# Gate and up tiles of the feed-forward stages: high weights times high and low activations in one 512-column product, the two parts added on VectorE

## The reference, cut to what matters

```python
def swiglu(h, wg, wu, wd):
    return (jax.nn.silu(h @ wg) * (h @ wu)) @ wd

for i in range(DEPTH):                         # DEPTH = 2
    ...
    x = x + swiglu(rms_norm(x, norm_ffn[i]), ffn_gate[i], ffn_up[i], ffn_down[i])
```

## Time and profile before

| | |
|---|---|
| median of 3 runs | 935.57 us (933.26 to 937.48) |
| the profiled execution | 935.31 us, its span 933.4 us |
| mean granted TensorE clock | 0.998 |
| PE busy | 914.7 us, 98% of the span, 7053 matmuls |
| DVE busy | 608.3 us, 65% |
| ACT busy | 485.7 us, 52% |
| POOL busy | 215.2 us, 23% |

### The profile page before, as it was taken

The page is one execution under the profiler, slowest core; times in us unless marked ns, Lnnn a source line. Parts: engine busy times, 40 slices in busy tenths (PEclk is TensorE's granted clock), DMA queues, the critical chain, the costliest instruction groups (busy, mean ns, idle before and its releaser), DMA issues.

```text
span 933.4 us, 17115 instructions
## 1 busy us (share of the span) xinstructions
PE 914.7 (98%) x7053; PEld 842.3 (90%) x7053; DVE 608.3 (65%) x827; ACT 485.7 (52%) x729; POOL 215.2 (23%) x177
## 2 busy tenths in 40 slices
PE   9999999999999999999999999999899999999998
PEld 8999999999999798899999997788788888899997
DVE  5876554554589999764545557746574756867664
ACT  6346434434465476744444346465556565547452
POOL 0005990000024230000000001316462704930100
PEclk9999999999999999999999999999999999999999
DMA  8765865666654522465656574546355635563461
GB/s 272 225 227 161 282 204 187 205 194 212 204 185 149 176 97 91 136 225 187 218 180 211 194 228 165 182 147 202 123 176 183 195 115 181 183 208 109 131 231 45
DMA packets 119636, 168.73 MB, mean 181 GB/s; under 512 B 5557, under 2 KB 88597, under 8 KB 119573
## 3 DMA queue, kind: packets, MB, share of 16 engines
q1 hardware_dynamic: 119140, 167.66, 55.5%
q10 hardware_dynamic: 432, 0.19, 0.1%
HBM read 165.38 MB, written 2.46 MB: 180 GB/s over the span
## 4 chain that ended last, share of the span: by engine, by line
PE 74%; DVE 14%; POOL 4%; ACT 3%; DMA 2%; issue 2%; SPq 0%; ACTq 0%; DVEq 0%; POOLq 0%
PE ps L480 21%; PE ps L482 21%; PE ps L481 21%; DVE wlo_sb L445 4%; POOL b_inv_sb L2477 3%; PE ps L922 2%; DMA raw_sb<-w_in_even 2%; PE ps L908 2%; PE ps L935 2%; DVE scratch_sb L1522 2%; ACT whi_sb L422 1%; POOL scratch_sb L2485 1%; PE ps L568 1%; DVE b_ss_sb L2319 1%; PE ps L2097 1%
## 5 line engine op out<-in xcount | busy, mean ns | idle before, releaser
L445 DVE TENSOR_TENSOR wlo_sb<-raw_sb,whi_sb 128x2048 fp32r<-128x2048 f32 x143 | 332.1, 2324 | 182.8 <-ACT whi_sb L422 182.7
L422 ACT ACTIVATE whi_sb<-raw_sb 128x2048 fp32r<-128x2048 f32 x143 | 273.6, 1914 | 161.8 <-PE ps L482 144.7
L480 PE MATMUL ps<-hhi_sb,whi_sb 128*128 128x256 f32 x992 | 274.1, 276 | 2.2 <-DVE wlo_sb L445 1.8
L481 PE MATMUL ps<-hlo_sb,whi_sb 128*128 128x256 f32 x992 | 272.8, 275 | 0.0
L482 PE MATMUL ps<-hhi_sb,wlo_sb 128*128 128x256 f32 x992 | 272.8, 275 | 0.0
L480 PEld LDWEIGHTS ps<-hhi_sb,whi_sb 128*128 128x128 f32 x992 | 190.4, 192 | 4.1 <-DVE wlo_sb L445 2.3
L481 PEld LDWEIGHTS ps<-hlo_sb,whi_sb 128*128 128x128 f32 x992 | 190.4, 192 | 0.5
L482 PEld LDWEIGHTS ps<-hhi_sb,wlo_sb 128*128 128x128 f32 x992 | 190.5, 192 | 0.0
L480 PE MATMUL ps<-whi_sb,hhi_sb 128*128 128x512 f32 (+2 forms) x304 | 115.7, 381 | 0.9 <-DVE wlo_sb L445 0.5
L482 PE MATMUL ps<-whi_sb,hlo_sb 128*128 128x512 f32 (+2 forms) x304 | 112.8, 371 | 0.0
L481 PE MATMUL ps<-wlo_sb,hhi_sb 128*128 128x512 f32 (+2 forms) x304 | 112.6, 370 | 0.0
(11 more groups left out here) (335 smaller groups left out, 1340.8 us busy)
## 6 DMA issues: line engine op xcount, KB each, us to landing
raw_sb<-w_in SPq DMA_DIRECT2D x45, 1024.0 KB, 5.2
raw_sb<-ffn_gate SPq DMA_DIRECT2D x22, 1024.0 KB, 5.3
raw_sb<-ffn_up SPq DMA_DIRECT2D x22, 1024.0 KB, 5.3
raw_sb<-ffn_down SPq DMA_DIRECT2D x22, 1024.0 KB, 4.9
raw_sb<-w_in_even SPq DMA_DIRECT2D x8, 1024.0 KB, 8.4
raw_sb<-w_in_odd SPq DMA_DIRECT2D x8, 1024.0 KB, 5.2
raw_sb<-w_branch SPq DMA_DIRECT2D x6, 1024.0 KB, 5.2
scratch_sb<-bias_rows_dram SPq DMA_DIRECT2D x40, 128.0 KB, 3.2
```

The source lines that it names most:

```text
L422: nc.scalar.activation(place(whi, n0), in_raw(n0), ACT.Copy).then_inc(hi_ready, 1)
L445: nc.vector.tensor_tensor(place(wlo, n0), in_raw(n0), place(whi, n0).bitcast(F32), ALU.subtract).then_inc(lo_ready, 1)
L480: nc.tensor.matmul(dst, l_hi, r_hi, start=first, stop=False)
L481: nc.tensor.matmul(dst, l_hi, r_lo, start=False, stop=False)
```

## The change

`hhi` and `hlo` become the two halves of one buffer `hboth`. In gate and up tiles of steps 1 to 10 the products whi x hhi and whi x hlo become one matmul of 512 columns whose streaming operand takes the 256 columns of `hhi` and then those of `hlo` (`both_parts`); wlo x hhi stays, 256 columns added to the first half of the result. For each half f and k there are so two matmuls in place of three. A result now fills a bank per half f: gate tiles use banks 6 and 7, up tiles 4 and 5, in every step. The second halves of the banks hold the part from `hlo`, and VectorE adds the two parts with a reduce over pairs (`two_sums`): gate into `sg`, up into `gu`. Silu then works in place on `sg` in SBUF, behind the split of tile g + 3, and VectorE multiplies `gu` by `sg` in SBUF. The up tile of step 10 is excepted: it keeps three products per f and k, with one bank per half, and its product on VectorE reads the banks. Step 0 is as before. TensorE waits, ahead of a gate or up tile of steps 2 to 10, for the sum of the tile of its kind in the step before (`summed`); the wait for `gu_ready` goes. `turn_first` uses bank 3.

```diff
--- before.py
+++ after.py
@@ -144,8 +144,8 @@
         wlo = sb("wlo", [P, (SPLIT - 1) * TILE + KC * WIDE], F32R)
 
         x = sb("x", [P, NT, D + 2])
-        hhi = sb("hhi", [P, KC, T], F32R)
-        hlo = sb("hlo", [P, KC, T], F32R)
+        hboth = sb("hboth", [P, 2, KC, T], F32R)
+        hhi, hlo = hboth[:, 0, :, :], hboth[:, 1, :, :]
         yhi = sb("yhi", [P, KC, T], F32R)
         ylo = sb("ylo", [P, KC, T], F32R)
 
@@ -344,6 +344,7 @@
         vec_landed, ident_landed, pw_landed = sem("vec_landed"), sem("ident_landed"), sem("pw_landed")
         gu_T = sem("gu_T")
         silu_ready, gu_ready, gu_hi, gu_lo = sem("silu_ready"), sem("gu_ready"), sem("gu_hi"), sem("gu_lo")
+        summed = sem("summed")
         stored = sem("stored")
 
         s_ready, s_shifted, p_ready, pT_ready, pT_copied, pv_done, o_copied = (
@@ -770,6 +771,10 @@
             w = a["ffn_gate" if kind == "g" else "ffn_up"][l]
             return w.rearrange("(k p) n -> p k n", p=P)[:, :, bass.ds(c * FFC, FFC)]
 
+        def sums(l, c):
+
+            return (2 * FSTEPS - 3) * l + 2 * (c - 1)
+
         def steps_of(engine, step, tail):
 
             step(0, 0)
@@ -795,17 +800,21 @@
 
         def ffn_act(act, l, n):
             def step(c, i):
-                g, b = g_tile(n, c), 4 + 2 * (c % 2)
+                g = g_tile(n, c)
                 split_hi(act, g + 2, i)
                 if c == 1:
                     act.wait_ge(gu_T, l + 1)
-                    nc.scalar.activation(ghi[:, 0, :, :], ps[:, 4, :].rearrange("p (f t) -> p f t", f=2),
+                    nc.scalar.activation(ghi[:, 0, :, :], ps[:, 3, :].rearrange("p (f t) -> p f t", f=2),
                                          ACT.Copy).then_inc(gu_hi, 1)
-                act.wait_ge(tile_used, i * 6 + (g + 1))
-                nc.scalar.activation(plain(sg[:, c % 2, :, :].rearrange("p f t -> p (f t)"), P), unmixed(ps[:, b, :], P),
-                                     ACT.Silu).then_inc(silu_ready, 1)
-                if c:
+                half = sg[:, c % 2, :, :]
+                if c == 0:
+                    act.wait_ge(tile_used, g + 1)
+                    nc.scalar.activation(plain(half.rearrange("p f t -> p (f t)"), P), unmixed(ps[:, 4, :], P),
+                                         ACT.Silu).then_inc(silu_ready, 1)
+                else:
                     split_hi(act, g + 3, i)
+                    act.wait_ge(summed, i * 4 + (sums(l, c) + 1))
+                    nc.scalar.activation(half, half, ACT.Silu).then_inc(silu_ready, 1)
                 if c < FSTEPS - 1:
                     split_hi(act, g + 3 + (1 if c else 0), i)
                 if c:
@@ -814,20 +823,39 @@
             steps_of(act, step, lambda: split_hi(act, n + 33))
 
         def ffn_dve(dve, l, n):
+            def two_sums(dst, bank):
+                parts = ps[:, bank:bank + 2, :].rearrange("p f (h b a) -> p f a b h", h=2, a=2)
+                return nc.vector.tensor_reduce(dst.rearrange("p f (a b) -> p f a b", a=2), parts, AX.X, ALU.add)
+
             def step(c, i):
-                g, b = g_tile(n, c), 4 + 2 * (c % 2)
+                g = g_tile(n, c)
                 split_lo(dve, g + 2, i)
                 if c == 1:
                     dve.wait_ge(gu_hi, FSTEPS * l + 1)
-                    nc.vector.tensor_tensor(glo[:, 0, :, :], ps[:, 4, :].rearrange("p (f t) -> p f t", f=2),
+                    nc.vector.tensor_tensor(glo[:, 0, :, :], ps[:, 3, :].rearrange("p (f t) -> p f t", f=2),
                                             ghi[:, 0, :, :].bitcast(F32), ALU.subtract).then_inc(gu_lo, 1)
                 if c:
+                    dve.wait_ge(tile_used, i * 6 + (g + 1))
+                    two_sums(sg[:, c % 2, :, :], 6).then_inc(summed, 1)
                     split_lo(dve, g + 3, i)
-                dve.wait_ge(silu_ready, i * 2 + (FSTEPS * l + c + 1))
                 dve.wait_ge(tile_used, i * 6 + (g + 2))
-                nc.vector.tensor_tensor(plain(gu[:, c % 2, :, :].rearrange("p f t -> p (f t)"), P),
-                                        plain(sg[:, c % 2, :, :].rearrange("p f t -> p (f t)"), P),
-                                        unmixed(ps[:, b + 1, :], P), ALU.mult).then_inc(gu_ready, 1)
+                up, half = gu[:, c % 2, :, :], sg[:, c % 2, :, :]
+                if c == FSTEPS - 1:
+                    dve.wait_ge(silu_ready, FSTEPS * l + c + 1)
+                    nc.vector.tensor_tensor(up.rearrange("p f (a b) -> p f a b", a=2),
+                                            half.rearrange("p f (a b) -> p f a b", a=2),
+                                            ps[:, 4:6, 0:T].rearrange("p f (b a) -> p f a b", a=2),
+                                            ALU.mult).then_inc(gu_ready, 1)
+                elif c:
+                    two_sums(up, 4).then_inc(summed, 1)
+                    dve.wait_ge(summed, i * 4 + (sums(l, c) + 2))
+                    dve.wait_ge(silu_ready, i * 2 + (FSTEPS * l + c + 1))
+                    nc.vector.tensor_tensor(up, up, half, ALU.mult).then_inc(gu_ready, 1)
+                else:
+                    dve.wait_ge(silu_ready, FSTEPS * l + 1)
+                    nc.vector.tensor_tensor(plain(up.rearrange("p f t -> p (f t)"), P),
+                                            plain(half.rearrange("p f t -> p (f t)"), P),
+                                            unmixed(ps[:, 5, :], P), ALU.mult).then_inc(gu_ready, 1)
                 if c < FSTEPS - 1:
                     split_lo(dve, g + 3 + (1 if c else 0), i)
                 if c:
@@ -845,9 +873,7 @@
                 mm_rows(t, ghi[:, c % 2, :, :], glo[:, c % 2, :, :], 0, first, False).then_inc(tile_used, 1)
 
             def step(c, i):
-                g, b = g_tile(n, c), 4 + 2 * (c % 2)
-                if c >= 2:
-                    pe.wait_ge(gu_ready, i * 2 + (FSTEPS * l + c - 1))
+                g = g_tile(n, c)
                 if c == 0:
 
                     first_part(pe, 2 * l + 1, n, 0, ps[:, 4, 0:FFC], 0, True, True, False)
@@ -856,25 +882,41 @@
                     first_part(pe, 2 * l + 1, n + 1, 0, ps[:, 5, 0:FFC], 0, True, True, True, True)
                     first_part(pe, 2 * l + 1, n, 0, ps[:, 4, FFC:2 * FFC], 1, True, True, False)
                     first_part(pe, 2 * l + 1, n + 1, 0, ps[:, 5, FFC:2 * FFC], 1, True, True, True)
-                for t, bank in ((g, b), (g + 1, b + 1)) if c else ():
+                for t, bank in ((g, 6), (g + 1, 4)) if c else ():
                     pe.wait_ge(lo_ready, i * 6 + (t + 1))
+                    if c >= 2:
+                        pe.wait_ge(summed, i * 4 + (sums(l, c - 1) + (1 if t == g else 2)))
                     hi, lo = w_parts(t, KC)
                     for f in range(2):
                         for k in range(KC):
                             cs = slice(f * P, f * P + P)
-                            mm = product(ps[:, bank, f * T:(f + 1) * T], hi[:, k, cs], lo[:, k, cs],
-                                         streams(hhi[:, k, :]), streams(hlo[:, k, :]), k == 0, k == KC - 1)
+                            if c == FSTEPS - 1 and t > g:
+                                mm = product(ps[:, bank + f, 0:T], hi[:, k, cs], lo[:, k, cs], streams(hhi[:, k, :]),
+                                             streams(hlo[:, k, :]), k == 0, k == KC - 1)
+                                continue
+                            if k:
+                                nc.tensor.matmul(ps[:, bank + f, 0:T], lo[:, k, cs], streams(hhi[:, k, :]), start=False,
+                                                 stop=False)
+                            mm = nc.tensor.matmul(ps[:, bank + f, :], hi[:, k, cs], both_parts(k), start=(k == 0),
+                                                  stop=(k == KC - 1))
+                            if k == 0:
+                                nc.tensor.matmul(ps[:, bank + f, 0:T], lo[:, k, cs], streams(hhi[:, k, :]), start=False,
+                                                 stop=False)
                         if c == 1 and t == g and f == 0:
                             turn_first(pe, l)
                     mm.then_inc(tile_used, 1)
                 if c and c < FSTEPS - 1:
                     down(c - 1, i, c == 1)
 
+            def both_parts(k):
+
+                return hboth[:, :, k, :].rearrange("p a (s b) -> p a b s", s=2)
+
             def turn_first(pe, l):
                 pe.wait_ge(gu_ready, FSTEPS * l + 1)
                 for i in range(NT):
                     for f in range(2):
-                        mm = nc.tensor.transpose(ps[:, 4, f * T + i * P:f * T + (i + 1) * P],
+                        mm = nc.tensor.transpose(ps[:, 3, f * T + i * P:f * T + (i + 1) * P],
                                                  gu[:, 0, i, f * P:(f + 1) * P], ident[:, :])
                 mm.then_inc(gu_T, 1)
 
```

## The result

The changed kernel takes 930.07 us (median of 5 runs, 929.38 to 931.13) against 935.57 us before on the same chip (5 runs there, 933.26 to 937.48). The ratio is 0.9945 with a 95% interval of 0.9925 to 0.9965. The forecast was 931.0 us, the range 928.6 to 934.8. The profiled execution took 929.95 us, its span is 928.1 us.

What follows compares the result with a forecast made beforehand. TensorE, busy without a gap in the feed-forward stages, was taken to bound the kernel. 608 merges of 7.4 ns save 4.5 us, other terms about zero: from 935.57 to 931.0 us, range 928.6 to 934.8.

Steps and rivals of the forecast that it cites:

- The merge: TensorE, gate and up tiles: two 256-column matmuls (223.28 ns) become one of 215.9; 7.4 ns each, 608 times, 4.5 us.
- Its two bounds: Merge gain on TensorE: 5.9 us if short products drop to 109.3 ns, 3.0 us if long ones take 218.3 ns.
- One sign of being wrong: TensorE in changed tiles: long products 0.22 us or more apart from their successor would show the forecast wrong.
- The rival of two streams at 111.6 each: TensorE: the merged product starts as two streams, each paying 111.6, so the merge saves little: 932.6 to 935.6 us; 16%.
- The sums and the gu product: VectorE: 1.22 us per sum, gu product about 0.69 us; a step rises from 8.25 to 10.7 us, covered by TensorE.
- the point where it would take over: VectorE in a step: from 3.7 us per sum it needs more than TensorE's 15.66 us; VectorE becoming the bound had 5%.
- New waits: TensorE ahead of gate and up tiles: each sum ends over 10 us before its banks are needed again; cost zero.
- The tight place: Step 1, first layer, late gate weights: low split ends at 107.7, TensorE comes at 108.8; one us left, cost zero.
- The end of a stage: Chain from the last up tile, left unmerged: the stage's gain passes on one to one; a longer gu product costs 0.1 us per layer.
- the 0.5% line: Whole kernel: bound for telling a change from none, at 930.9 us, almost on the forecast.
- the near-even split of chances: Whole kernel's outcome: 0.41 faster, 0.52 same, 0.07 slower.

Runs made afterwards that it cites:

- e1: Changed kernel with each 512-column product made as two of 256 columns again, sums, waits and banks kept: 934.26 us, ratio 0.9993 to the kernel before.
- e2: Changed kernel with eight long products, then eight short ones per half tile, in place of turns: 928.63 us, ratio 0.9933 to the kernel before.
- e3: Kernel before, with the low-weight product put in the middle of each three and cut to 64 of its 128 loaded columns: 933.34 us, ratio 0.9988.
- e6: Changed kernel with three more reduces over the same PSUM ahead of each sum: 965.89 us, ratio 1.0338 to the kernel before.
- e7: The changed kernel once more, unaltered: 929.09 us against 935.15 for the kernel before, ratio 0.9938.
- e4: Changed kernel with the last up tile of each stage merged too, its sum on VectorE: 931.61 us, ratio 0.9968 to the kernel before.

## Why the prediction was right

**The merge.** 7.4 ns by two rows of the trace, 7.5 measured (e1 against after); 4.5 us forecast, 608 x 7.5 ns = 4.56 us measured. Its two bounds (the long product pays the load, the short one gains by it) showed up in the records both at once, 218.5 and 109.2 ns, and cancel. That isn't luck in the sum: in turns as in groups (e2), each pair has one load under a short product. One sign of being wrong came close: 0.216 us behind a long product was named as right and 0.22 as wrong, and 0.218 was measured. The rival of two streams at 111.6 each, 223 together, is out. The cause that the prediction named, the load that paces short products, is supported by the sorted starts and by e3. The formula in the section "Back-to-back issue gap" of the Trainium skill's page "TensorE: Matmul & The Clock Gate", which the page calls the gap of an isolated matmul, makes an estimate of 2.5 ns per merge (2.6 in the prediction, from rounded gaps); the runs have 7.5, and the measurement decides.

**The sums and the gu product.** 1.22 us forecast, 1225 ns measured over 38, though there are 512 results where the row that it was taken from had four:

```profile
L828 DVE TENSOR_REDUCE scratch_sb<-ps 128x512 f32<-128x1024 f32 x38 | 46.5, 1225 | 33.9 <-PE ps L900 33.9
L853 DVE TENSOR_TENSOR scratch_sb<-scratch_sb 128x512 f32<-128x512 f32 x18 | 12.7, 705 | 2.1
```

In these two rows the time goes with the number of elements read, not with the number written. The gu product has 705 ns where about 690 were taken. VectorE's step was mis-sized slightly, 10.7 forecast and 10.53 us measured, as was the point where it would take over: 3.7 us per sum came from durations, which back to back overlap a little (e6).

**New waits.** None, as argued: with the sums, the single banks, the Silu behind the split and the two waits ahead of a tile, but without the merge, a stage was 0.07 us shorter than before (e1). The forecast had put these at nothing.

**The tight place.** The weights landed 1.40 us later still, and the margin, reckoned to be one us, held. ScalarE, VectorE and TensorE there answer to the earlier trace rows:

```profile
104.72 1.91 ACT L423 ACTIVATE whi_sb<-raw_sb 128x2048 fp32r<-128x2048 f32 x1 [7.05 <-DMA raw_sb<-ffn_gate]
```

```profile
106.66 2.29 DVE L446 TENSOR_TENSOR wlo_sb<-raw_sb,whi_sb 128x2048 fp32r<-128x2048 f32 x1 [5.74 <-ACT whi_sb L423]
...
110.12 0.77 DVE L853 TENSOR_TENSOR scratch_sb<-scratch_sb 128x512 f32<-128x512 f32 x1
110.81 2.28 DVE L446 TENSOR_TENSOR wlo_sb<-raw_sb,whi_sb 128x2048 fp32r<-128x2048 f32 x1
```

```profile
109.91 0.38 PE L900 MATMUL ps<-hboth_sb,whi_sb 128*128 128x512 f32 x1
```

The gate tile's low split ends at 106.66 + 2.29 = 108.95 and TensorE starts that tile at 109.91, so 0.96 us were left. The up tile's split ends at 113.09; the forecast was 111.9, plus 1.25 for the later start 113.2. TensorE started the stage 1.25 us later too, so it was hardly closer than reckoned. In e7, with an earlier start, the margin is 0.95 us, and no profile with the change has less than 0.58 (e4).

**The end of a stage.** 9.35 us before and after. e4 shows what the exception for the last up tile is worth: 1.14 us per layer.

**What the forecast left out.** The medians differ by 5.5 us, the stages by 4.57, and the 16 merges ahead of the cuts are worth another 0.12. Most of the rest is the half-clock stretch and the start, which vary by themselves. At equal clock 0 to 0.3 us are left outside the stages, less than these means can tell from zero, and in the median of e1 0.3 us with an interval that takes in zero; whether the change has a part in that stays open. So that the median came 0.9 us below the forecast is for the most part chance. The ratio of 0.9945 lies just beyond the 0.5% line, with an interval to both sides of it, as the near-even split of chances had it. One step of the prediction doesn't add up: 929.7 to 932.6 with 2 us to either side is 927.7 to 934.6, not 928.6 to 933.5. The measured 930.07 lies in both.

## What to carry to other kernels

Where an engine has no gap, take the distance of starts, not durations, and price a merge of two short products by the two distances that the trace already has; here that came within 0.1 us. Two products that share their stationary weights and have 256 columns each are worth joining where an engine has room to add the parts; leave out the tile whose sum would stand in the chain at a stage's end. Before a difference between two profiles is put down to a change, cut both into stages: what moves in a stage that the edit doesn't touch may be chance. A second profile of each kernel may not tell (both of before had the half-clock stretch); the clocks of many runs did.

## What the runs showed of the hardware

At a granted clock of 1.00 the distance from a product's start to the next one's hangs on its own columns and on those of the product ahead of it, under which its 128 x 128 load runs: 109 ns for 256 columns behind 512, 111.6 for 256 behind 256, 218.5 for 512 behind 256, 216 for 512 behind 512. A product of 256 columns behind 256, narrowed to 64 loaded columns, has 109 as well. A reduce over pairs out of PSUM, 1024 elements to 512, takes 1225 ns, as long as one of 1024 to four (1218). VectorE's instructions back to back start 0.08 to 0.09 us closer than they last (e6). And the same 2.4 us of waiting on TensorE was followed by the lower clock in seven profiles of ten (427 ns per 512 columns; in before 8 products, or 1.7 us, fewer in the 10 us) and by the full clock in three, one of them of a kernel whose other profile had the lower one.
